# Token-row gathers of a mixture-of-experts stage: empty places get an index beyond the last row, and the gathers get a bound

## The reference, cut to what matters

```
def grouped_expert_ffn(hf, eidx, gate, w1, w3, w2):   # hf: 1024 x 1024, eidx: 1024 x 2, 32 experts
    ...                                               # sort the 2048 (token, expert) pairs by expert
    def run_block(args):                              # one block: rows of one expert
        toks, gts, ei = args
        xb = hf[toks]                                 # gather of token rows, 1024 floats each
        hb = jax.nn.silu(xb @ w1[ei]) * (xb @ w3[ei])
        return (hb @ w2[ei]) * gts[:, None]
    ...
    return jax.ops.segment_sum(...)                   # add each token's two results
```

## Time and profile before

| | |
|---|---|
| median of 3 runs | 1596.22 us (1594.56 to 1597.02) |
| the profiled execution | 1597.23 us, of it 1595.4 us span from first to last instruction |
| TensorE busy | 1356.9 us (85% of the span) |
| DVE, ACT, GpSimd busy | 631.6, 385.7, 76.5 us |
| bytes moved | 331.40 MB |
| granted TensorE clock | mean 0.93 of full speed |

### The profile page before, as it was taken

The page is one execution under the profiler, slowest core; times in us unless marked ns, Lnnn a source line. Parts: engine busy times, 40 slices in busy tenths (PEclk is TensorE's granted clock), DMA queues, the critical chain, the costliest instruction groups (busy, mean ns, idle before and its releaser), DMA issues.

```text
span 1595.4 us, 17126 instructions
## 1 busy us (share of the span) xinstructions
PE 1356.9 (85%) x6271; PEld 689.7 (43%) x6271; DVE 631.6 (40%) x1400; ACT 385.7 (24%) x873; POOL 76.5 (5%) x109
## 2 busy tenths in 40 slices
PE   2899999999876888998899955999989898898750
PEld 2744444444564444544445533444434343343320
DVE  5726424422046676666423344222232222222307
ACT  2334211101065655554232320000000000000005
POOL 0000000000013000000000000000000000000013
PEclk8899999999987999999999965999999999999975
DMA  9611222112320870000362262999999999999957
GB/s 337 144 53 54 93 106 105 53 53 106 123 89 5 236 240 1 1 1 1 124 245 79 79 263 96 365 391 401 382 399 393 410 395 394 392 393 405 418 193 290
DMA packets 109979, 331.40 MB, mean 208 GB/s; under 512 B 26172, under 2 KB 50376, under 8 KB 101320
## 3 DMA queue, kind: packets, MB, share of 16 engines
q1 hardware_dynamic: 97400, 299.86, 50.2%
q0 software_dynamic: 5712, 19.42, 3.6%
q10 hardware_dynamic: 6784, 11.02, 1.9%
HBM read 287.78 MB, written 42.49 MB: 207 GB/s over the span
## 4 chain that ended last, share of the span: by engine, by line
PE 28%; SPq 17%; DVE 6%; DMA 4%; issue 2%; ACT 2%; DVEq 0%; POOL 0%; ACTq 0%
SPq L637 14%; PE ps L1411 6%; PE ps L1451 5%; PE ps L1501 4%; PE ps L1462 3%; DMA arena<-expert_w 2%; PE ps L1317 2%; PE ps L1334 2%; PE ps L1354 2%; SPq L635 2%; SPq L683 1%; ACT arena L998 1%; PE ps L1396 1%; PE ps L1441 1%; DMA d_y<-arena 1%
## 5 line engine op out<-in xcount | busy, mean ns | idle before, releaser
L1462 PE MATMUL ps<-arena 128*32 128x256 f32 (+1 forms) x1408 | 198.4, 501 | 34.1 <-DMA arena<-expert_w 31.8
L1172 PE MATMUL ps<-arena 128*128 128x512 f32 x512 | 221.0, 593 | 0.0
L1501 PE MATMUL ps<-arena 128*32 128x256 f32 (+2 forms) x832 | 152.7, 498 | 4.3 <-issue 1.9
L1172 PEld LDWEIGHTS ps<-arena 128*128 128x128 f32 x512 | 96.9, 190 | 119.7 <-issue 119.6
L1179 PE MATMUL ps<-arena 128*128 128x512 f32 (+1 forms) x384 | 142.0, 530 | 1.2 <-ACT arena L843 1.2
L1462 PEld LDWEIGHTS ps<-arena 128*32 128x32 f32 (+1 forms) x1408 | 74.9, 127 | 143.6 <-issue 126.6
L1451 PE MATMUL ps<-arena 128*128 128x512 f32 x256 | 116.7, 614 | 7.9 <-DVE arena L2006 7.9
L1411 PE MATMUL ps<-arena 128*128 128x512 f32 x256 | 112.7, 592 | 0.1
L998 ACT ACTIVATE arena<-arena 128x640 f32<-128x640 f32 (+7 forms) x128 | 92.8, 727 | 59.2 <-DVE arena L1808 59.2
L1179 PEld LDWEIGHTS ps<-arena 128*128 128x128 f32 x384 | 72.3, 189 | 68.9 <-issue 62.1
L1334 PE MATMUL ps<-arena 128*128 128x128 f32 x528 | 79.9, 285 | 21.2 <-ACT arena L998 9.2
(11 more groups left out here) (318 smaller groups left out, 1315.4 us busy)
## 6 DMA issues: line engine op xcount, KB each, us to landing
arena<-expert_w SPq DMA_DIRECT2D x99, 2048.0 KB, 35.4
arena<-ada_w SPq DMA_DIRECT2D x12, 2048.0 KB, 9.2
d_y<-arena SPq DMA_DIRECT2D x24, 512.0 KB, 6.3
arena<-x SPq DMA_DIRECT2D x16, 512.0 KB, 4.4
arena<-w_in SPq DMA_DIRECT2D x4, 2048.0 KB, 12.9
d_y<-arena ACTq DMA_DIRECT2D x40, 128.0 KB
arena<-w_out SPq DMA_DIRECT2D x2, 2048.0 KB, 14.0
d_x<-arena SPq DMA_DIRECT2D x8, 512.0 KB, 2.6
```

Of the source, the lines that this page charges most:

```text
L1172: last = nc.tensor.matmul(b, w(k), hT[:, k, 512 * c:512 * c + 512], start=(k == 0), stop=(k == KT - 1))
L1462: last = nc.tensor.matmul(ps[width * j:width * j + width, 2 if width == 64 else 3, 0:span], xgT[s][:, k, lo:lo + width], w_up[slots[n]][:, ...
L1501: last = nc.tensor.matmul(dst, hid_T[s][:, at_:at_ + width], w_down[slot][:, k, span * j:span * j + span], start=(k == 0), stop=(k == 3))
```

## The change

Empty places get the index 2048 instead of 0. To get there, `tok_id` runs from -2048 upward, so a held place sums to token - 2048 and an empty one stays 0, and 2048 is added to the whole table where it leaves PSUM. Both gathers of token rows get a bound of 1023 and don't treat an index beyond it as an error. The rows of `xg` for empty places then keep what stood there. The gathers of result rows at the end are unchanged, and so are the blocks' sizes, the matmuls and the weight loads.

```
-            nc.gpsimd.iota(tok_id, [[P, NT]], base=0, channel_multiplier=1, allow_small_or_imprecise_dtypes=True)
+            nc.gpsimd.iota(tok_id, [[P, NT]], base=-2 * S, channel_multiplier=1, allow_small_or_imprecise_dtypes=True)
...
                 pool.indirect_dma_start(xg[q % 2][0:rows, :], None, d_xn,
-                                        bass.IndirectOffsetOnAxis(ap=row_tok[0:rows, place:place + 1], axis=0)).then_inc(xg_in[q % 2], 16)
+                                        bass.IndirectOffsetOnAxis(ap=row_tok[0:rows, place:place + 1], axis=0),
+                                        bounds_check=S - 1, oob_is_err=False).then_inc(xg_in[q % 2], 16)
...
                 pool.indirect_dma_start(xg[s], None, d_xn,
-                                        bass.IndirectOffsetOnAxis(ap=idx_col[s], axis=0)).then_inc(xg_in[s], 16)
+                                        bass.IndirectOffsetOnAxis(ap=idx_col[s], axis=0),
+                                        bounds_check=S - 1, oob_is_err=False).then_inc(xg_in[s], 16)
...
-            read(V.tensor_copy(row_tok, b[:, 0:NB]), "table")
+            read(V.tensor_scalar(row_tok, b[:, 0:NB], float(2 * S), None, ALU.add), "table")
```

## The result

The changed kernel takes 1587.28 us (median of 4, 1586.05 to 1588.12) against 1596.62 us before (median of 4, 1594.56 to 1598.46): a ratio of 0.9945, 95% interval 0.9929 to 0.9961, so the gain is clear of the noise. The forecast was 1589.5 us in a range of 1582.5 to 1597.5; the gain is 9.3 us by the medians where 6.7 was worked out.

What follows compares the result with a forecast made beforehand. From 1135 to 1464 us the byte stream was taken as the bound, with TensorE waiting 31.1 us for weights. Terms +0.1 - 4.4 - 0.3 - 2.1 = -6.7 us on 1596.2 gave 1589.5 us, range 1582.5 to 1597.5.

Steps and rivals of the forecast that it cites:

- (a): Token table ahead of the first gather: its copy out of PSUM becomes an add, 0 to +0.1 us, taken +0.1.
- (b): Steps 13 to 31, bound by the byte stream: 455 empty rows, 1.86 MB, no longer carried, taken as 4.4 us gain.
- (d): Rate lost around gathers below 128 rows: 371 empty rows give back 0 to 7.1 us, taken 2.1.
- (c): Steps 3 to 12, where the load queue waits for slots: 76 empty rows, 0 to 0.7 us gain, taken 0.3.
- the slope: Growth of a gather's rate loss with its rows, 0.0116 us a row; for 371 empty rows 4.3 us.
- (e): Cost of the bound on gathers, only the first gather being uncovered: taken 0, bounds 0 and 5.4 us.
- (f): First gather's landing with 67 rows of 128 instead of all: at most 0.6 us gain, taken 0.
- (g): Overflow block and tail: 11 empty rows worth nothing; a 12.45 us result-store landing sets the chain and shifts along.
- Rival 1: Gathers of empty places: the lanes decide what a skipped row gives back; bytes fall but time doesn't; chance 0.20.
- Rival 2: Gathers: nothing is skipped, indexes beyond the bound still make packets, bytes and packets stay, 1596.3 us; chance 0.08.
- Rival 3: First gather, uncovered: the bound costs time, cancelling the gain at 6.7 us, 1602.3 us at 100 ns a row; chance 0.12.
- Rival 4: More gain than counted: (d) in full, 7.1 us, plus (b), (c) and (f), 12.8 us, 1583.4 us; chance 0.08.

Runs made afterwards that it cites:

- e5: Changed kernel plus ten small VectorE operations whose result is thrown away, as control for e6: 1590.76 us, ratio 0.9966 to the kernel before.
- e6: Changed kernel plus ten small VectorE operations that spread a block's tokens evenly over its lanes, same rows skipped: 1589.91 us, ratio 0.9965 to the kernel before.
- e1: Kernel before, nothing skipped, but empty places read row 7 x lane instead of row 0: 1597.43 us, ratio 1.0005.
- e2: Kernel before with only the bound added to both gathers; empty places still read row 0: 1595.68 us, ratio 0.9992.
- e10: e8 without the bound and without the table's offset, so nothing is skipped: 1581.87 us, ratio 0.9909 to the kernel before.
- e8: e7 with the tokens of every second 64-row place put into lanes 64 to 127: 1569.64 us, ratio 0.9836 to the kernel before.
- e3: Changed kernel with all static gathers in the 128-partition shape, lanes beyond the block's rows skipped: 1580.63 us, ratio 0.9887 to the kernel before.
- e4: Kernel before with all static gathers in the 128-partition shape, no bound, nothing skipped: 1583.88 us, ratio 0.9918.
- e7: e3 run again, beside e8 on the same chip: 1578.10 us, ratio 0.9882 to the kernel before.
- e9: Changed kernel with 4096 instead of 2048 added to the table, so all token-row gathers are skipped: 1554.15 us, ratio 0.9732 to the kernel before.

## Why the prediction was right, and which term was too small

- *What bounds the kernel.* Right: all of TensorE's gain comes after step 13's transpose, in the part fed by the weight stream; its waits for weights fell by 9.4 us.
- *(a) table.* Taken at +0.1, measured 0 (0.22 us both times).
- *(b) bytes of steps 13 to 31.* Taken in full, 4.4 us. e5 and e6 show that it didn't depend on lanes, and e1 and e2 that it wasn't the repeated row or the bound. It can't be separated from (d) in this kernel, so the full 4.4 stays an assumption; the pair e10 and e8 shows nearly the full value for skipped bytes, in the other shape.
- *(c) bytes of steps 3 to 12.* Taken at 0.3, and more came of it. TensorE sets the pace up to step 13 and gains only 0.1 us there, but the load queue was running ahead: SP's pair of load issues that started at 1148.58 us before starts at 1146.74 after, 1.84 us earlier. TensorE's first long wait for weights (in brackets), before and after:

```profile
1181.49 8.56 PE L1462 MATMUL ps<-arena 128*64 128x512 f32 x32 [5.42 <-DMA arena<-expert_w]
```

```profile
1178.04 8.78 PE L1464 MATMUL ps<-arena 128*64 128x512 f32 x32 [2.04 <-DMA arena<-expert_w]
```

  The other traces agree: 5.25 and 4.80 us in e1 and e2, which skip nothing, 2.27 and 2.07 in e5 and e6, which skip. The difference here is 3.4 of the 9.7 us, when of the 19 gathers counted in (b) and (d) only those of steps 13 and 14 had landed. So part of what the gathers up to step 12 saved, in bytes and in rate, was kept as a lead of the load queue and paid out here. The forecast left their rate out and took less than half of their bytes.
- *(d) the loss of rate.* This is the term that was mis-sized most. I took half of the slope, 2.1 us. The part lost 21.0 us of rate before and loses 329 x (1 - 404/423) = 14.8 after, so it gave 6.2 us; by the timeline, 9.7 - 4.4 = 5.3, and that still holds what (c) paid out. The full slope, 4.3, would have been near it: halving it, because of the spread inside one size, is what failed. The proportional bound of 7.1 is too high. With the full slope the sum would have been 8.9 us; that it would then meet 9.3 is in part luck, as (b) and (c) aren't measured apart.
- *(e) the bound.* Taken at 0 with 5.4 us as its upper bound. The first transpose comes 0.7 us later after the table than before (6.80 against 6.11), of which 0.06 is shown to be the bound's, and the stage started 1.35 us later by scatter. Of this, 1.5 us was left at step 1's transpose (1002.31 against 1000.85), and that was made up by TensorE's clock. Windows around the up-projection of step 1 (columns as in the earlier trace rows), before and after:

```profile
1003.80:1009.00 5.20, 5.15 (x65) 2.44 (x65) 0.59 (x1) 0.00 (x0) 0.00 (x0) 0.69 1.00 367
```

```profile
1001.00:1004.00 3.00, 2.96 (x16) 1.68 (x14) 1.28 (x4) 0.00 (x0) 0.00 (x0) 1.00 0.65 209
1003.80:1009.00 5.20, 3.85 (x67) 2.06 (x66) 2.05 (x8) 0.00 (x0) 0.91 (x1) 1.00 0.98 351
```

  Before, the granted clock is 0.69 on average over step 1's up-projection, after it is 1.00. By step 2's transpose both kernels are level: 1008.98 and 1008.90 us. This was luck of the profiled executions and no effect of the change: from step 1's transpose to step 2's it is 8.1 us in the traces of the kernel before, e3, e4 and e7 (clock 0.67 to 0.73 in that window) and 6.6 in those of the changed kernel, e1, e2, e5, e6, e8, e9 and e10 (clock 1.00), with and without a bound on both sides.
- *(f), (g).* The landing of the first gather got no shorter: TensorE waited 6.84 us for it, 6.16 before. The 12.45 us store wait of the earlier trace rows became 12.77, so the tail in essence only shifted.
- *Rivals.* Rival 1, that the lanes decide, to which the prediction gave 0.20, doesn't hold in the kernel that was changed (e5 and e6, 0.9966 and 0.9965), and does hold in the 128-partition shape (e7 and e8, 8.5 us apart by the medians). Rival 2 was half right in mechanism, as the packets stay, and wrong in what counts, as the bytes go. Rival 3 looked at the right place; the price there is at most 0.7 us, where 6.7 would have cancelled the gain. Rival 4's 12.8 us wasn't reached: (f) gave nothing and (d) less than 7.1.

The experiments also leave a kernel that beats both: e8, 1569.64 us, 26 us below the kernel before.

## What to carry to other kernels

When a stage is bound by its DMA stream, look at the rate around small transfers before counting their bytes: here the 25 gathers of fewer than 128 rows cost more by their shape than by the rows that were empty, and asking for all 128 partitions, with more bytes, was the larger gain (13 us against 9). Skipping entries by a bound saved bytes here but not packets (16.80 MB instead of 19.42, 5,712 packets both times), and with the 128-partition shape it paid nearly in full only where the skipped lanes changed from one gather to the next: 11.7 of 13.2 us, against 4 to 6 where they didn't. Why is not shown. And a lead of the load queue can hold a saving that the compute engine shows only later: SP's issues stood 1.84 us earlier, and TensorE's first long wait for weights then fell from 5.42 to 2.04 us.

## What the runs showed of the hardware

- A gathered row beyond the bound still makes a packet, of under 512 bytes: 5,712 packets with and without, 640 more under 512 B; 2,688 of them, in gathers that move no row at all, cost no rate (420 GB/s).
- A bound on a gather costs nothing that can be told over the kernel (0.9992), and 0.06 us up to the end of the first gather's instruction; TensorE's wait for that gather scatters by more than any price seen.
- Gathers into 32, 64 or 96 partitions slow the whole DMA stream (396 GB/s on average of the weight-bound part), and the same rows asked for in a 128-partition gather hardly do (417 to 420). In that part packets take longer, those of the weights too (40.3 against 38.5 us of an engine for a megabyte). Few partitions alone are not the reason: e3 writes its 64-row blocks into the same 64 partitions, at 417 GB/s. What in the smaller shape is, these runs leave open.
- Reading the same 4 KB row 640 times is as fast as reading other rows, over the kernel (1.0005, 0.9991 to 1.0020).
